# Three moves of a write, a score step and a key load around the sample attention of a hybrid decoder layer

## The reference

```python
# sample attention: 8 new rows of queries against 2048 cached keys and values of each sample
kall = jnp.concatenate([buf_k, k], axis=1)      # cache_win_k, then the 8 new rows
vall = jnp.concatenate([buf_v, v], axis=1)
for win, dil in PATTERNS:                        # (128,1), (512,4), (2048,16)
    s = einsum('bshe,bskhe->bhsk', q, kall[:, idxc]) + bias
    pr = exp(s - max(s));  o = einsum('bhsk,bskhe->bshe', pr, vall[:, idxc]) / den
# routing: rows are sorted into blocks of 128 slots by expert; an empty slot names the row T
slot_tok = jnp.full((n_blk * MOE_BLK,), T).at[dest].set(tok)
slot_w = jnp.zeros((n_blk * MOE_BLK,)).at[dest].set(wts)
```

## Time and profile before

| what | value |
|---|---|
| median of three runs | 2416.71 us |
| the profiled execution: time, span | 2403.83 us, 2402.2 us |
| TensorE (PE) busy | 2166.7 us, 90% of the span |
| VectorE (DVE) busy | 852.5 us, 35% |
| ScalarE (ACT) busy | 562.8 us, 23% |
| GpSimd (POOL) busy | 284.8 us, 12% |
| mean DMA traffic | 183 GB/s |
| chain that ended last, by engine | PE 77%, DVE 9%, DMA 5%, issue 4%, ACT 2% |

### The profile page before, as it was taken

One profiled execution on the slowest core, in us unless ns is written; L12 is line 12 of the kernel. 1 busy time (PEld: TensorE's weight loads), 2 busy tenths in 40 slices (PEclk: granted clock), 3 DMA queues, 4 the chain that ended last, 5 costly groups with the idle time before them and its releaser, 6 DMA issues.

```text
span 2402.2 us, 27992 instructions
## 1 busy us (share of the span) xinstructions
PE 2166.7 (90%) x7615; PEld 1092.0 (45%) x7616; DVE 852.5 (35%) x1969; ACT 562.8 (23%) x1110; POOL 284.8 (12%) x463
## 2 busy tenths in 40 slices
PE   3996999999989899999599299999999999999995
PEld 1343555544545665656244144444444444444342
DVE  3566554014572455565365511111111111111112
ACT  3410010225532434443122111111111111111111
POOL 0001020100010000001222211111111111111111
PEclk8998999999999589999899599999999999999998
DMA  9253131431546522223754635774479788687873
GB/s 376 93 215 60 54 70 54 169 98 70 136 161 192 180 65 104 100 91 139 246 209 156 216 128 162 274 251 150 155 262 335 268 325 321 215 309 270 308 251 70
DMA packets 122756, 438.91 MB, mean 183 GB/s; under 512 B 31955, under 2 KB 70579, under 8 KB 102115
## 3 DMA queue, kind: packets, MB, share of 16 engines
q1 hardware_dynamic: 92520, 309.99, 35.2%
q0 software_dynamic: 26032, 112.64, 17.4%
q10 hardware_dynamic: 4112, 15.14, 1.6%
HBM read 356.39 MB, written 83.10 MB: 183 GB/s over the span
## 4 chain that ended last, share of the span: by engine, by line
PE 77%; DVE 9%; DMA 5%; issue 4%; ACT 2%; POOL 1%; SPq 1%; DVEq 0%; ACTq 0%; POOLq 0%
PE bank L2550 20%; PE bank L2191 12%; PE bank L2578 10%; PE bank L2455 7%; PE bank L2554 4%; PE bank L2299 3%; PE bank L2354 3%; PE bank L2331 2%; PE bank L2581 2%; PE bank L2516 2%; PE bank L2341 2%; PE bank L2303 1%; PE bank L2271 1%; DMA arena<-xT 1%; DMA arena<-kc 1%
## 5 line engine op out<-in xcount | busy, mean ns | idle before, releaser
L2550 PE MATMUL bank<-arena 128*128 128x512 f32 x1120 | 491.0, 595 | 14.7 <-issue 14.7
L2191 PE MATMUL bank<-arena 128*128 128x512 f32 (+1 forms) x960 | 359.0, 533 | 9.6 <-ACTq L1066 9.6
L2550 PEld LDWEIGHTS bank<-arena 128*128 128x128 f32 x1120 | 211.9, 190 | 289.8 <-issue 289.8
L2578 PE MATMUL bank<-arena 128*128 128x512 f32 x560 | 249.6, 598 | 11.4 <-issue 11.2
L2191 PEld LDWEIGHTS bank<-arena 128*128 128x128 f32 x960 | 168.4, 191 | 193.9 <-issue 193.0
L2455 PE MATMUL bank<-arena 128*128 128x512 f32 x512 | 243.1, 599 | 0.0
L2083 DVE COPY arena<-bank 128x512 f32<-128x512 f32 x50 | 34.6, 693 | 550.3 <-PE bank L2565 550.3
L2578 PEld LDWEIGHTS bank<-arena 128*128 128x128 f32 x560 | 103.0, 189 | 135.1 <-issue 125.9
L2093 DVE TENSOR_TENSOR arena<-bank,arena 128x512 f32<-128x512 f32 (+1 forms) x50 | 34.5, 691 | 255.6 <-PE bank L2578 210.7
L2455 PEld LDWEIGHTS bank<-arena 128*128 128x128 f32 x512 | 87.8, 191 | 75.9 <-issue 75.8
L985 POOL DMA_INDIRECT o_y<-arena x50 | 79.3, 1586 | 307.5 <-issue 171.0
(11 more groups left out here) (475 smaller groups left out, 2562.2 us busy)
## 6 DMA issues: line engine op xcount, KB each, us to landing
arena<-wg SPq DMA_DIRECT2D x32, 2048.0 KB, 9.4
arena<-wu SPq DMA_DIRECT2D x32, 2048.0 KB
arena<-wd SPq DMA_DIRECT2D x32, 2048.0 KB, 8.1
arena<-mod_w SPq DMA_DIRECT2D x12, 2048.0 KB, 17.8
z_d<-arena ACTq DMA_DIRECT2D x12, 1056.0 KB, 6.4
arena<-z_d POOLq DMA_DIRECT2D x10, 1056.0 KB, 7.7
arena<-kc POOLq DMA_DIRECT2D x8, 1280.0 KB, 10.0
arena<-vc POOLq DMA_DIRECT2D x8, 1280.0 KB, 8.4
```

What stands on the lines that cost most here:

```text
L2191: ins = mm(bank[n % 2][:, 0:w], wz[:, i % 3, k, :], hT[:, k, t0:t0 + w], start=(k == 0), stop=(k == KT - 1))
L2550: ins = mm(bank[bk][:, :], xgT[:, s, k, :], m[w][:, k, :], start=(k == 0), stop=(k == KT - 1))
L2578: ins = mm(bank[4 + h][:, :], hhT[:, k, :], wd[w][:, k, 512 * h:512 * h + 512], start=(k == 0), stop=(k == 3))
```

## The change

The default list is placed in the gate rows' region (s5_at + 3072) and is made and written in step "smp", in front of the load of the gate rows, with a wait for its two writes on GpSimd. `rinit` no longer makes it, and "ts" no longer waits for it; "ts" waits for the end of the attention's units instead, as `rinit` does. In the table of offsets the first pair's score steps go from 4, 5, 6 to 0, 1, 2. All later sample steps, but for the offset of "ts", go one step forward (the first pair of the second half, for instance, from 18 to 17). The keys of samples 2 and 3 are issued at offset 3 and the values of samples 0 to 2 at offset 4; before they were at 7 and 1.

```diff
-        dflt = take(4 * (NBLK - 1), h_at).bitcast(I32).rearrange("p (b w) -> p b w", w=4)
+        dflt = take(4 * (NBLK - 1), s5_at + 3072).bitcast(I32).rearrange("p (b w) -> p b w", w=4)
...
-        for f, hf, first in (("sS", 0, (4, 9)), ("sS", 1, (18, 25)), ("sV", 0, (17, 22)), ("sV", 1, (33, 38))):
+        for f, hf, first in (("sS", 0, (0, 8)), ("sS", 1, (17, 24)), ("sV", 0, (16, 21)), ("sV", 1, (32, 37))):
...
-        for hf, b, t, o in ((0, 10, 14, 25), (1, 26, 30, 41)):
+        for hf, b, t, o in ((0, 9, 13, 24), (1, 25, 29, 40)):
...
-        for n, f, bs in ((-4, "kc", (0, 1)), (1, "ts", ()), (1, "vc", (0, 1, 2)), (7, "kc", (2, 3)), (12, "kc", (4, 5)), (20, "vc", (3, 4)),
-                         (21, "kc", (6, 7)), (25, "vc", (5, 6)), (36, "vc", (7,))):
+        for n, f, bs in ((-4, "kc", (0, 1)), (1, "ts", ()), (3, "kc", (2, 3)), (4, "vc", (0, 1, 2)), (11, "kc", (4, 5)), (19, "vc", (3, 4)),
+                         (20, "kc", (6, 7)), (24, "vc", (5, 6)), (35, "vc", (7,))):
...
                 pool.wait_ge(S("att_o"), AT["att_o"] + 3)
                 pool.dma_start(nrow, A["nffn"].broadcast_to([P, D])).then_inc(S("ld_rows"), 16)
+                link(pool.memset(dflt, 0))
+                link(pool.iota(dflt[:, :, 1], pattern=[[0, NBLK - 1]], base=T, channel_multiplier=1))
+                pool.dma_start(tok_v[:, 0:NBLK - 1, :], dflt).then_inc(S("st_dflt"), 16)
+                pool.dma_start(tok_v[:, NBLK - 1:NBLK, :], dflt[:, 0:1, :]).then_inc(S("st_dflt"), 16)
+                pool.wait_ge(S("st_dflt"), 32)
...
             def sample_bias(step, bs):
-                pool.wait_ge(S("st_dflt"), 32)
+                pool.wait_ge(S("att_pT"), AT["att_pT"] + NU)
+                pool.wait_ge(S("att_pv"), AT["att_pv"] + NU)
...
             def rinit(step):
                 pool.wait_ge(S("att_pT"), AT["att_pT"] + NU)
                 pool.wait_ge(S("att_pv"), AT["att_pv"] + NU)
-                link(pool.memset(dflt, 0))
-                link(pool.iota(dflt[:, :, 1], pattern=[[0, NBLK - 1]], base=T, channel_multiplier=1))
-                pool.dma_start(tok_v[:, 0:NBLK - 1, :], dflt).then_inc(S("st_dflt"), 16)
-                pool.dma_start(tok_v[:, NBLK - 1:NBLK, :], dflt[:, 0:1, :]).then_inc(S("st_dflt"), 16)
```

## The result

The changed kernel takes 2403.99 us (median of seven runs, 2397.86 to 2406.32); the kernel before took 2416.71 us in the same rounds (2410.77 to 2420.88). The ratio is 0.9948, with a 95% interval of 0.9934 to 0.9962: 12.7 us faster, where 27 were forecast. The time lies inside the range given, 2379 to 2406, near its slow end.

What follows compares the result with a forecast made beforehand. TensorE bounds nearly everywhere, with a hole of 24.03 us waiting for late keys. Terms 0 + 20.0 (keys) + 0.5 (clock) + 5.0 + 1.5 (ScalarE waits) = 27.0 us off 2416.7 gave 2390, range 2379 to 2406.

Steps and rivals of the forecast that it cites:

- GpSimd's timeline: After the attention, GpSimd starts the bias table at about 1137.6, 5.9 us sooner, and issues the keys at 1146.2, 9 sooner.
- first scores in time: First pair's scores start on PE at 1134.53, four steps sooner, with their keys already there.
- margin of the scores: First scores end at about 1143.3, before GpSimd asks at 1146.2: 3 us of margin, no wait.
- when PE asks: PE wants the second pair's keys at 1156.1, one projection step of 1.99 us before the old 1158.1.
- That GpSimd's list is what the keys wait for: Keys of samples 2 and 3 go out late for GpSimd's list, not for the scores that free their buffers, done at 1151.5.
- When the keys land: wait of 4 us: Second pair's keys land at 1160; PE waits 4 us instead of 24.03, gain 20.0 (bounds 16.5 to 24.0).
- rival A: Keys stay late, SyncE's loads taking turns with them: wait 7.5 to 12 us, 15 us gained, 2402; chance 0.17.
- The clock behind the hole: PE's matmuls after the key wait run slow, 2.0 us lost; remaining wait still costs 1.5, gain 0.5 (0 to 2.0).
- The two waits for ScalarE, gain 6.5: PE's waits of 4.54 and 2.13 us for copies of transposes go: gains 5.0 and 1.5, bounds together 0 to 8.1.
- Everything else one step forward: Later key and value loads keep their distance in steps to their users: 0 us (-2 to 0).
- The default list at its new place, 0 to 1: List made before the gate rows beside the attention delays them 9.5 us with 30 to spare: cost 0, bounds 0 to 1.
- Rival B: VectorE's list or the mixers' rows bound next: PE loses 5 to 9 us, copy gains go, 19 us gained, 2398; chance 0.12.

Runs made afterwards that it cites:

- e1: Changed kernel with the default list made and written in rinit again, at its old place; 2400.27 us, ratio 0.9939 to the kernel before.
- e4: Changed kernel with the bias table issued behind the keys of samples 2 and 3, ahead of the values; 2400.62 us, ratio 0.9941 to the kernel before.
- e7: Changed kernel with the bias table loaded by 4 DMAs of 32 rows instead of 16 of 8; 2395.62 us, ratio 0.9924 to the kernel before.
- e8: Changed kernel with SyncE's three loads of the samples' gate rows two row tiles later; 2399.43 us, ratio 0.9932 to the kernel before.
- e6: Changed kernel with all sample steps but first pair's scores, keys 2 and 3, values 0 to 2 at old offsets; 2401.50 us, ratio 0.9943 to before.
- e9: Changed kernel with the exponential step of each half one step back; 2396.38 us, ratio 0.9938 to the kernel before.
- e10: Changed kernel with the bias table in 4 pieces and the gate rows two tiles later; 2400.24 us, ratio 0.9950 to the kernel before.
- e12: Changed kernel with table in 4 pieces, gate rows later and exponentials one step back; 2394.83 us, ratio 0.9925 to the kernel before.
- e13: Changed kernel with table in 4 pieces and exponentials one step back, gate rows unmoved; 2389.88 us, ratio 0.9899 to the kernel before.

## Why the prediction was wrong

- *GpSimd's timeline, first scores in time, margin of the scores, when PE asks, list hidden behind 302 us of idleness*: right, each with its number in the trace after (keys issued 11.8 us after the release, 11.4 forecast).
- *That GpSimd's list is what the keys wait for*: right in the kernel before only in part. Once the values no longer stand ahead, the time of the issue doesn't decide: in e1 it is 5.2 us later and the keys reach PE no later.
- *When the keys land: wait of 4 us*: wrong, and the step that failed. 15.1 us were measured, above the bound of 7.5 and above the 10 that the prediction names as a sign that it is wrong. The keys took 21.0 to 23.9 us from their issue, where the forecast had 13 and the bound 16.9. The bound subtracted the values ahead at 3.1 us each and kept the rest of the old landing time. But the keys then start earlier into the same slow stretch, and their landing moves little with their issue (e1); it is set by what is in flight ahead of them, the table (e4, e7) and the gate rows (e8). I had the table's 1 MB in GpSimd's issue time alone, 8 us, and never as a load in front of the keys; the row with a landing of 10 us for a 64 KB piece at 1150 was in the view of the kernel before. The shortfall is 11 us. In rival A the size was nearer (7.5 to 12), and the mechanism, turns with SyncE's loads, is half of it. That its 2402 us is near the 2404 measured is partly luck: it leaves the table out, has a wait 3 us too short, and a gain at ScalarE that didn't come. The Trainium skill's sentence on turns between queues (page "DMA: Bandwidth & Descriptors", section "Queues, rings and completion order") was the right warning. This case agrees so far as loads on SyncE's queue held keys on GpSimd's queue (9.0 us less wait in e8); no run shows that the turns go by packets. I priced it by the loads issued at 1150 alone, without the 768 KB issued at 1143.
- *The clock behind the hole*: a gain of 0.5 was forecast. Behind the hole 3.63 and 2.68 us were taken where 1.91 and 1.99 are full speed, 2.4 us lost; before the change it was 2.0 (3.63 and 2.29). So it cost 0.4 us more than before.
- *The two waits for ScalarE, gain 6.5*: the mechanism was right, and both waits are gone (8.1 us with the clock). The 0 (-2 to 0) for "Everything else one step forward" was wrong: I followed the one copy that the step let pass, and not the exponential, which the same step put ahead of the merge's copy. 1.64, 4.18, about 1.8 of slow matmuls behind the latter and 1.45 for a sample's new rows make 9.1. The net is -1 for 6.5. The exchange is shown by e6, the exponential's part in it by e9.
- *The default list at its new place, 0 to 1*: there is a wait of 2.35 us at 832, VectorE behind a store of att_d that shares its time with the gate rows, now issued at 822.6. It is in all twelve profiles with the early list (2.2 to 2.7) and in none of the four with the late one, so the early list brings it, though which transfer holds the store wasn't tested. As the attention stage differs by 9 us between executions anyway, what it costs in the end isn't told.
- *The sum for the sample stretch*: forecast 27.0, measured 10.5, so 16.5 are missing. The keys account for 11.1, ScalarE for 7.5 and the clock for 0.9, which is 19.5. The other 3 us came back in waits that the prediction didn't name: 1.60 us became 0.66 at L2433 and 5.43 became 4.31 at L2487, and the rest is in smaller differences. The median moved by 12.7.
- *Rival B*: its own terms, 5 to 9 us lost and the 6.5 of the copies gone, leave 11.5 to 15.5 of the 27 and not the 19 that it states. That would be 2401 to 2405, where the result lies, but half of that is luck. PE did lose 9 us in new places, most of it behind an exponential that waits for VectorE's maximum; but the two copy gains, which B has going, came, and what B keeps, a key wait of 4, did not.

## What to carry to other kernels

A load that is issued earlier lands earlier only if what delays its landing was the issue: before pricing it, list everything that is in flight ahead of it on all queues, small pieces above all, with its landing times. When a step moves in a program made of in-order lists, look at each engine's instruction that moved, and ask for each what now stands behind it. And a wait that is removed entirely isn't always worth more than one that is made short: e10 and e12, without a key wait, are slower in the sample stretch than e7 and e13, which keep 4 us of it, since moving the gate rows brought another wait and VectorE's list took over. e13 came to 24.8 us below the kernel before in its rounds, for 27 forecast, by other means than the prediction's.

## What was not expected of the hardware

- DMA engines at a share of 0.85 to 1.07 moved 147 to 173 GB/s with the table's pieces in flight (1150 to 1166), and 413 behind them. Which packets were slow isn't settled: the cut into 16 pieces was worth 10.7 us of wait (2.9 of it issue time), the gate rows 9.0, and these overlap; a shifted source 3.6, which is within the spread of single profiles.
- Of sixteen loads of 8 rows of 8 KB the median one landed 4.3 us after its issue and the last 17.3, 28.5 us after the release. Of four loads of 32 rows, the same bytes, the median was 8.3 and the last 10.6, some 16 us after the release; 5.5 of the 12 us between them is GpSimd's time to issue.
